# Two-block transformer kernel on one core: block 2's first norm with its mean taken off early and its squares summed as the output projection comes

## The reference

```python
mix = jnp.concatenate([a_out, b_out], axis=-1) @ w_o[i]
x = layer_norm(ALPHA * x + mix, ln1_g[i], ln1_b[i])
gate, up = jnp.split(x @ w_ffn_in[i], 2, axis=-1)
...
ple = (p[i] @ w_ple[i]) * jax.nn.sigmoid(x @ w_ple_gate[i])
x = layer_norm(ALPHA * x + ffn + ple, ln2_g[i], ln2_b[i])
...
def layer_norm(x, g, b):
    mu = jnp.mean(xf, axis=-1, keepdims=True)
    var = jnp.mean(jnp.square(xf - mu), axis=-1, keepdims=True)
    y = (xf - mu) * lax.rsqrt(var + LN_EPS)
```

## Time and profile before

| | us |
|---|---|
| median of 3 runs (2494.79 to 2498.84) | 2498.53 |
| profiled execution, its own time | 2500.13 |
| its span in the trace | 2498.3 |
| PE busy | 2424.8 (97%) |
| DVE busy | 1765.1 (71%) |
| ACT busy | 1095.0 (44%) |
| POOL busy | 1065.5 (43%) |
| granted TensorE clock, mean | 0.992 |

### The profile page before, as it was taken

One profiled execution on the slowest core, in us unless ns is written; L12 is line 12 of the kernel. 1 busy time (PEld: TensorE's weight loads), 2 busy tenths in 40 slices (PEclk: granted clock), 3 DMA queues, 4 the chain that ended last, 5 costly groups with the idle time before them and its releaser, 6 DMA issues.

```text
span 2498.3 us, 35167 instructions
## 1 busy us (share of the span) xinstructions
PE 2424.8 (97%) x13615; PEld 2033.0 (81%) x13615; DVE 1765.1 (71%) x2671; ACT 1095.0 (44%) x1803; POOL 1065.5 (43%) x600
## 2 busy tenths in 40 slices
PE   6999999999999999999999999999999999999997
PEld 4777788988777788998777779999877777999985
DVE  4677777864477787774597478887468747888746
ACT  4325532434426543443444555444444355444442
POOL 0323553434234244544254446544515534755441
PEclk8999999999999999999999999999999999999998
DMA  8613345553322433332232113332223212333221
GB/s 288 203 51 123 114 152 169 189 164 110 95 85 85 135 118 119 102 102 85 86 85 76 55 64 127 108 104 92 95 82 85 76 51 68 102 124 105 94 87 49
DMA packets 239645, 268.87 MB, mean 108 GB/s; under 512 B 19976, under 2 KB 204024, under 8 KB 239224
## 3 DMA queue, kind: packets, MB, share of 16 engines
q1 hardware_dynamic: 239480, 266.63, 33.1%
HBM read 264.51 MB, written 2.10 MB: 107 GB/s over the span
## 4 chain that ended last, share of the span: by engine, by line
PE 75%; DVE 10%; issue 5%; ACT 4%; POOL 3%; DMA 3%; SPq 1%; ACTq 0%; DVEq 0%; POOLq 0%
PE bank L2801 22%; PE bank L2803 22%; PE bank L2802 22%; DVE k_lo L2057 1%; DMA raw<-in_w_ffn_in 1%; DVE r L1908 1%; POOL w_lo L1652 1%; POOL k_lo L1663 1%; DMA raw<-in_ffn_w 1%; ACT k_hi L1105 1%; DVE u_sum L2074 1%; PE bank L3404 1%; PE bank L3470 1%; DVE u_t_raw L2087 1%; PE bank L3130 1%
## 5 line engine op out<-in xcount | busy, mean ns | idle before, releaser
L1663 POOL TENSOR_TENSOR k_lo<-raw,k_hi 128x512 fp32r<-128x512 f32 x297 | 430.0, 1459 | 542.9 <-ACT k_hi L1105 541.9
L1652 POOL TENSOR_TENSOR w_lo<-raw,w_hi 128x2048 fp32r<-128x2048 f32 x53 | 248.8, 4694 | 525.3 <-ACT w_hi L1051 446.3
L1105 ACT ACTIVATE k_hi<-raw 128x512 fp32r<-128x512 f32 x444 | 270.9, 626 | 310.7 <-PE bank L2803 249.4
L2801 PE MATMUL bank<-h_hi,k_lo 128*128 128x256 f32 (+1 forms) x1156 | 370.8, 321 | 3.8 <-DVE k_lo L2057 2.5
L2802 PE MATMUL bank<-h_lo,k_hi 128*128 128x256 f32 (+1 forms) x1156 | 369.6, 320 | 0.0
L2803 PE MATMUL bank<-h_hi,k_hi 128*128 128x256 f32 (+1 forms) x1156 | 369.5, 320 | 0.0
L2801 PE MATMUL bank<-h_hi,w_lo 128*128 128x512 f32 x800 | 325.0, 406 | 10.7 <-DVE h_lo L2017 3.9
L2803 PE MATMUL bank<-h_hi,w_hi 128*128 128x512 f32 x800 | 313.4, 392 | 0.0
L2802 PE MATMUL bank<-h_lo,w_hi 128*128 128x512 f32 x800 | 313.3, 392 | 0.0
L2801 PE MATMUL bank<-f_hi,k_lo 128*128 128x512 f32 x704 | 278.4, 395 | 8.6 <-DVE u_row L2118 2.9
L2801 PE MATMUL bank<-u_t_hi,k_lo 128*128 128x256 f32 x1008 | 282.6, 280 | 1.2 <-POOL k_lo L1663 1.2
(11 more groups left out here) (401 smaller groups left out, 4929.6 us busy)
## 6 DMA issues: line engine op xcount, KB each, us to landing
raw<-in_ffn_w SPq DMA_DIRECT2D x56, 1024.0 KB, 5.4
raw<-in_w_ffn_in SPq DMA_DIRECT2D x44, 1024.0 KB, 5.1
raw<-in_w_in SPq DMA_DIRECT2D x34, 1024.0 KB
b_raw<-in_ada_w SPq DMA_DIRECT2D x32, 1024.0 KB, 5.2
f_raw<-in_w_ffn_out SPq DMA_DIRECT2D x24, 512.0 KB, 3.4
z_a<-in_ada_w SPq DMA_DIRECT2D x4, 2048.0 KB, 14.1
g_raw<-in_ada_w SPq DMA_DIRECT2D x8, 1024.0 KB, 5.6
raw<-in_w_out SPq DMA_DIRECT2D x8, 1024.0 KB
```

The source lines that it names most:

```text
L1105: act.activation(hi, src, ACT.Copy).then_inc(s.f_hi.up, 1)
L1652: pool.tensor_tensor(b.w_lo[p][:, 0:n], b.raw[p][:, 0:n], b.w_hi[p][:, 0:n].bitcast(F32), ALU.subtract)\
L1663: pool.tensor_tensor(lo, src, hi.bitcast(F32), ALU.subtract).then_inc(s.f_lo.up, 1)
L2801: pe.matmul(out, wlo, xhi, start=start, stop=False)
```

## The change

Three things change in each layer of block 2.

1. DVE adds up the eight tiles of `x` before the last half of the output projection comes (`dve_early_shift`, seven additions), PE sums that over channels right behind the first channel tile of `attended(0)`, and DVE takes this provisional mean off all eight tiles; only then come the additions of the projection's tiles.
2. ACT squares each tile as soon as its addition is done, between its splits 14 and 15. PE sums the squares of tiles 0 to 3 between output tiles 6 and 7, those of 4 to 6 behind tile 7, and that of tile 7 at the end.
3. The variance is the mean square less the squared mean: ACT squares the mean, DVE subtracts, ACT goes on with `Ln` and `Exp`. The remaining mean is taken off tile by tile between the scalings.

```diff
@@ act_layer_norm
-    for k in range(KD):
-        act.wait_ge(*s.ld(l, k + 1))
-        act.activation(b.sq[:, k, :], b.x[:, k, :], ACT.Square).then_inc(s.lsq.up, 1)
     act.wait_ge(*s.lmean(l, 2))
-    act.activation(b.r[:, :], bank[7][:, :], ACT.Ln, bias=b.eps[:, 1:2], scale=1.0 / D).then_inc(s.l_r.up, 1)
-    act.wait_ge(*s.l_r(l, 1))
+    act.activation(b.sq[:, 1, :], bank[6][:, :], ACT.Square, scale=1.0 / D).then_inc(s.l_r.up, 1)
+    act.wait_ge(*s.var(l, 1))
+    act.activation(b.r[:, :], b.sq[:, 1, :], ACT.Ln, bias=b.eps[:, 1:2]).then_inc(s.l_r.up, 1)
+    act.wait_ge(*s.l_r(l, 2))
     act.activation(b.r[:, :], b.r[:, :], ACT.Exp, scale=-0.5).then_inc(s.l_r.up, 1)
     act_normed(act, e, l * 2, 0)
+
+def act_square_out(act, e, l, ks):
+    s, b = e.s, e.b
+    for k in ks:
+        act.wait_ge(*s.res(l, k + 1))
+        act.activation(b.sq[:, k, :], b.x[:, k, :], ACT.Square).then_inc(s.lsq.up, 1)
@@ act_layer2
     split(14)
+    act_square_out(act, e, l, range(KD))
     split(15)
     act_layer_norm(act, e, l)
@@ dve_layer_norm
-    dve.wait_ge(*s.lmean(l, 1))
-    for k in range(KD):
-        dve.scalar_tensor_tensor(b.x[:, k, :], bank[6][:, :], -1.0 / D, b.x[:, k, :], ALU.mult, ALU.add)\
-           .then_inc(s.ld.up, 1)
-    dve.wait_ge(*s.l_r(l, 2))
-    for k in range(KD):
-        dve.wait_ge(*s.ld(l, k + 1))
+    dve.wait_ge(*s.l_r(l, 1))
+    dve.wait_ge(*s.lmean(l, 3))
+    dve.scalar_tensor_tensor(b.sq[:, 1, :], bank[7][:, :], 1.0 / D, b.sq[:, 1, :], ALU.mult, ALU.subtract)\
+       .then_inc(s.var.up, 1)
+    for k in range(2):
+        dve_less_mean(dve, e, k, -1.0 / D)
+    dve.wait_ge(*s.l_r(l, 3))
+    for k in range(KD):
+        dve.wait_ge(*s.ld(l, KD + k + 1))
         dve_scaled(dve, e, k)
         if k == 0:
             dve_normed(dve, e, l * 2, 0)
+        if k + 2 < KD:
+            dve_less_mean(dve, e, k + 2, -1.0 / D)
...
+def dve_less_mean(dve, e, k, part):
+    s, b = e.s, e.b
+    dve.scalar_tensor_tensor(b.x[:, k, :], e.bank[6][:, :], part, b.x[:, k, :], ALU.mult, ALU.add)\
+       .then_inc(s.ld.up, 1)
+
+def dve_early_shift(dve, e, lay, l):
+    s, b = e.s, e.b
+    for k in range(2):
+        dve.wait_ge(*lay.bank_out(k % 2, PART_USE[KD - 2 + k]))
+    dve.tensor_tensor(b.r[:, :], b.x[:, 0, :], b.x[:, 1, :], ALU.add).then_inc(s.lsum.up, 1)
+    for k in range(2, KD):
+        dve.wait_ge(*s.lsum(l, k - 1))
+        dve.tensor_tensor(b.r[:, :], b.r[:, :], b.x[:, k, :], ALU.add).then_inc(s.lsum.up, 1)
+    dve.wait_ge(*s.lmean(l, 1))
+    for k in range(KD):
+        dve_less_mean(dve, e, k, -1.0 / D)
@@ dve_layer2
     c = l * 2
+    dve_early_shift(dve, e, lay, l)
     for k in range(KD):
+        dve.wait_ge(*s.ld(l, k + 1))
         dve.wait_ge(*(s.att(l, 3 * (k // 4) + k % 4 + 1) if k % 4 < 3 else
                       s.tile(lay.pair(6), k // 4, 1)))
-        dve.wait_ge(*lay.bank_out(k % 2, PART_USE[k]))
@@ pe_layer_norm
-    pe.wait_ge(*s.lsum(l, 6))
+    pe_square_sums(pe, e, l, range(4, KD - 1))
+    pe.wait_ge(*s.lsum(l, 13))
+    pe.wait_ge(*s.ld(l, KD))
     pe.matmul(bank[6][:, :], b.ones[:, :], b.r[:, :], start=True, stop=False)
     pe.wait_ge(*s.res(l, KD))
     pe.matmul(bank[6][:, :], b.ones[:, :], b.x[:, KD - 1, :], start=False, stop=True).then_inc(s.lmean.up, 1)
-    for k in range(KD):
+    pe_square_sums(pe, e, l, (KD - 1,)).then_inc(s.lmean.up, 1)
+
+def pe_square_sums(pe, e, l, ks):
+    s, b = e.s, e.b
+    for k in ks:
         pe.wait_ge(*s.lsq(l, k + 1))
-        op = pe.matmul(bank[7][:, :], b.ones[:, :], b.sq[:, k, :], start=(k == 0), stop=(k == KD - 1))
-    op.then_inc(s.lmean.up, 1)
+        op = pe.matmul(e.bank[7][:, :], b.ones[:, :], b.sq[:, k, :], start=(k == 0), stop=(k == KD - 1))
+    return op
@@ pe_layer2, attended
                     if k == 3:
                         op.then_inc(*((s.att.up, 1) if m < 3 else (s.half.up, 2)))
+                if k == 0:
+                    pe.wait_ge(*s.lsum(l, KD - 1))
+                    pe.matmul(bank[6][:, :], b.ones[:, :], b.r[:, :], start=True, stop=True).then_inc(s.lmean.up, 1)
...
                 op.then_inc(*((s.att.up, 1) if m < 7 else (s.half.up, 2)))
+                if m == 6:
+                    pe_square_sums(pe, e, l, range(4))
```

More of the change, by code:

```diff
@@ L598, in __init__ @@
         self.gn_m, self.v_m = in_turn("gn_m_v_m", 2, 1)
-        self.gn_x, self.lsum = in_turn("gn_x_lsum", 2, 6)
+        self.gn_x, self.lsum = in_turn("gn_x_lsum", 2, 13)
         self.cn_x, self.wi = in_turn("cn_x_wi", 2, 1)
@@ L639, in __init__ @@
         self.v_n = up("v_n", 4)
-        self.lmean = up("lmean", 2)
-        self.ld = up("ld", 8)
-        self.l_r = up("l_r", 2)
+        self.lmean = up("lmean", 3)
+        self.ld = up("ld", 2 * KD)
+        self.l_r = up("l_r", 3)
         self.n2_sum = up("n2_sum", 3 + 6)
@@ L646, in __init__ @@
         self.n2_r = up("n2_r", 3)
-        self.n2_var = up("n2_var", 1)
+        self.var = up("var", 2)
         self.lxr = up("lxr", KD + 1)
@@ L1401, in act_shift_norm @@
     act.activation(b.f_full[:, 1, :], bank[6][:, :], ACT.Square, scale=1.0 / D).then_inc(s.n2_r.up, 1)
-    act.wait_ge(*s.n2_var(l, 1))
+    act.wait_ge(*s.var(l, 2))
     act.activation(b.r[:, :], b.f_full[:, 1, :], ACT.Ln, bias=b.eps[:, 1:2]).then_inc(s.n2_r.up, 1)
@@ L2479, in dve_add_up @@
     else:
-        dve.wait_ge(*s.lsum(l, k - 1))
+        dve.wait_ge(*s.lsum(l, k + 6))
         dve.tensor_tensor(b.r[:, :], b.r[:, :], b.x[:, k, :], ALU.add).then_inc(s.lsum.up, 1)
@@ L2542, in dve_shift_norm @@
     dve.scalar_tensor_tensor(b.f_full[:, 1, :], bank[7][:, :], 1.0 / D, b.f_full[:, 1, :], ALU.mult, ALU.subtract)\
-       .then_inc(s.n2_var.up, 1)
+       .then_inc(s.var.up, 1)
     for k in range(2):
```

## The result

| | before | changed |
|---|---|---|
| median of the compared runs, us | 2497.75 (4 runs) | 2518.26 (4 runs, 2516.99 to 2521.16) |
| ratio | | 1.0086, 95% interval 1.0068 to 1.0103 |
| profiled execution, its own time, us | 2500.13 | 2518.86 |
| its span, us | 2498.3 | 2517.1 |

The change makes the kernel 20.5 us slower. The forecast was 23.1 us slower, 2521.6; the range was 2509 to 2528. The profiled spans differ by 18.8 us only: the changed execution reached the norm 2.7 us earlier than the one before (DVE's last probabilities start at 1405.3 against 1408.0), which is nothing that the change does. I therefore compare stretches inside each execution, not start times.

A forecast was written before the change was run, and what follows sets the result against it. The prediction took PE, busy 97% of the span, as the bound. Per layer 7.1 + 1.7 + 3.4 - 0.65 = 11.55 us, 23.1 for two, giving 2521.6 us against the 2498.5 median; range 2509 to 2528.

The forecast's parts named there:

- Term A: At attended(0), PE waits for DVE's seven additions, held up by POOL, then sums: 7.1 us a layer, 6.1 idle.
- DVE wins the last turn: Rival: addition 7 enters before POOL's split 13, PE idles 1.7 us, the early sum costs 2.8; 2509.6 us; chance 0.06.
- POOL does not hold the additions up: Rival: the seven additions end before PE asks, leaving 0.95 us for the sum; 2501.9 us in all; chance 0.06.
- Term B: Behind PE's wait for the early sum, the lower clock costs 1.7 us a layer (1.7 or 2.5 possible).
- Term C: Four sums of squares on PE ahead of output tile 7, 0.86 us each: 3.4 us a layer.
- Term D: From last projection matmul to the gate's second channel tile: gain of 0.65 us a layer, 2.2 without clock loss.
- The norm itself pays: Rival: the square sums and early sum find idle PE slots, leaving a 2.65 us gain a layer; 2493.2 us; chance 0.03.

The follow-up runs named there:

- Experiment 2: Changed kernel with 25 discarded matmuls in front of PE's wait for the early sum: 2515.65 us, ratio 1.007.
- Experiments 1: Changed kernel with the running sum of the early additions in a PSUM bank, so all but the first have one SBUF input: 2506.17 us, ratio 1.0035.
- experiment 9: experiment 8 with ACT writing the inverse root into PSUM bank 7, from where DVE scales: 2490.07 us, ratio 0.9972.
- experiment 11: experiment 10 with the early mean back, gathered in PSUM and summed on PE behind the second channel tile: 2492.26 us, ratio 0.9979.
- experiment 4: Changed kernel with PE's early sum behind the third channel tile of attended(0) instead of the first: 2504.42 us, ratio 1.003.
- experiment 6: Changed kernel without early additions, early sum or early subtraction; squares are of x with its mean in it: 2501.49 us, ratio 1.0016.
- experiment 8: Changed kernel without early mean, split 15 before tile 7's square, fp32r square sums, 26 discarded matmuls ahead of the wait replacing 19 behind: 2491.80 us, ratio 0.9975.
- experiment 7: Kernel before, with squares written as fp32r and summed with fp32r ones, one pass instead of two: 2495.83 us, ratio 0.9993.
- experiment 10: experiment 9 with each h_lo earlier in DVE's list, ahead of later mean subtractions, and 20 discarded matmuls instead of 26: 2490.94 us, ratio 0.9971.
- experiment 5: Changed kernel with ACT's split 15 ahead of the square of tile 7 instead of behind it: 2518.61 us, ratio 1.0085.
- experiments 3: Changed kernel with all eight sums of squares behind output tile 7, none ahead of it: 2517.36 us, ratio 1.0078.

## Why the prediction was right, point by point

**Term A, the early sum (7.1 forecast): right, and shown.** The wait is 5.62 us (6.1 forecast), released by DVE's last addition, in both layers. The turns came out one by one as worked from the earlier trace rows: additions 3, 4, 6 and 7 were held, 1, 2 and 5 were not. Experiment 2, where the clock stays up, has the term alone: 23.46 us from the twelfth projection matmul to the slot behind tile 6 instead of 16.55, so 6.91. Addition 7 lost its turn to split 13, so the rival *DVE wins the last turn* fell. Experiments 1 and 9 show that POOL is the cause. That rules out the rival *POOL does not hold the additions up*, and with it the narrow reading of the Trainium skill's "Advanced Engine Details and Errata", section "VectorE Performance Modes". Another page of the Trainium skill, "SBUF — State Buffer", section "Who interferes with whom", says that a DVE instruction with two SBUF inputs contends with a GpSimd instruction that reads SBUF, and one with at most one SBUF input, outside the 2-port modes, does not. The trace agrees on both: 1.65 to 4.98 us against 0.7.

**Term B, the clock behind it (1.7 forecast): right in kind, too small.** Experiment 2 gives 2.45 and 2.68 us in the trace, about the upper of my bounds; I had taken the value of a shorter stretch. The slow time did begin while PE was still idle (granted clock 0.50 from 1420.4, the sum starts at 1421.98), but 5.1 us of it were left for the matmuls. A and B together were forecast at 8.8. From the twelfth projection matmul to the slot behind tile 6 they cost 9.24 us in the first layer (25.79 instead of 16.55) and 9.47 in the second.

**Term C, four sums ahead of tile 7 (3.4): right.** Tile 7 is 3.44 us later in the trace. Up to the first matmul behind the sums it is 3.03 us; another 0.4 passes because the second fp32r matmul behind them comes 0.63 us after the first, not 0.23. Together that is the four times 0.86. The early sum costs the same where PE doesn't wait for it: in experiment 11 the stretch from the twelfth projection matmul to the slot behind tile 6 takes 17.45 us instead of 16.55, so 0.90, and for that part of term A I had 0.96. In experiment 4 it takes 18.02, so 1.47, because there PE still waits: the sum starts at 1424.07, where the next projection matmul was due at 1423.61. The medians of experiments 4 and 6 differ by 2.9, 1.5 a layer.

**Term D, the tail (gain of 0.65 forecast): mis-sized.** It gained 2.29 and 2.27 us in the two layers of the profiled execution. The step that failed is "I take 1.7 us for it", the lower clock behind the idle stretch of 2.85. The stretch came (2.80), the lower clock did not, and without it I had worked out 2.2. The other kernels show why neither value is the answer: behind the same stretch the clock fell in five of ten layers, for 1.3 to 1.6 us each. By these ten layers the right term is a gain of about 1.5 us on average, an estimate, with both values in the range. What decides between the two stays open.

**The sum.** In the profiled execution 9.24 + 3.44 - 2.29 = 10.4 us in the first layer and 10.6 in the second, 21.0 for two; the medians differ by 20.5. Forecast 23.1: 1.6 a layer too much in D, 0.5 too little in A and B. The two errors have opposite signs, so part of the closeness is luck. By whole runs it comes apart like this: squares and tail alone 4.0 us (experiment 6), the early sum with next to no wait 2.9 more (experiment 4), the wait 11.2 more (experiment 2), the clock 2.6 more (changed kernel), with some of D's chance in each figure.

**The norm itself pays** was the rival with a gain. Experiment 6 puts the norm without its early mean at 4 us slower, so it falls as stated: the sums found no idle slots. It is the price of the sums on PE that decides: with sums at a quarter of the price, split 15 ahead of the last square and the idle stretch filled, the norm without its early mean is 5.7 us faster than the kernel before (experiment 8), while the old form gains nothing certain by them (experiment 7).

**The best version** of these is experiment 9, 2490.07 us, ratio 0.9972; 8 and 10 can't be told from it. With the early mean kept, it is experiment 11, 0.9979. All four sum the squares in fp32r, with the lower precision that experiment 7 names.

## What to carry to other kernels

Before work is moved under another engine's work, look at where its inputs lie and what GpSimd does at that time: a chain of VectorE operations with two SBUF inputs can take three times its length, and one input in PSUM frees it. Put a wait on an in-order engine only where the last thing that it waits for is certain to be done; two channel tiles later, the same slow additions cost their sum and a wait of 0.30 us. When one part gets earlier, ask what other engines then start earlier, and what that runs into (experiment 10). And an idle stretch of PE of 2.3 to 2.9 us has had two prices here, with and without the lower clock behind it: carry both.

## What the runs showed of the hardware that I had not expected

- Behind an idle stretch of 2.73 to 2.81 us in one and the same place the granted clock fell in five of ten layers, in some executions in one layer and not in the other. Behind 2.32 and 2.33 us at another place it fell in three of four (experiments 10 and 11). Behind 1.55 and 1.56 us it stayed at 1.00 (experiment 5), and in a wait of 5.59 to 5.63 it fell in all six layers of the changed kernel and of experiments 3 and 5 (the early sum behind it took 2.07 or 2.08 us instead of 1.12).
- The clock also fell with no idle stretch of that length at all: in experiment 7, where PE started a short matmul every 0.6 us with pauses between them, it was 0.62 during the sums.
- A `tensor_scalar` with one SBUF input and its output in SBUF, 0.55 us alone, took 0.95 and ended 0.27 us behind POOL's operation (experiment 9), as the two-input operations do with 0.55. The Trainium skill's page "SBUF — State Buffer", section "Who interferes with whom", lists `tensor_scalar` among the operations that can take the ports which DVE and GpSimd share; the trace agrees. `scalar_tensor_tensor` with a PSUM input was not held up (0.69 for one and 1.28 for two beside POOL in experiment 9).
- Behind an fp32 sum the second of the fp32r matmuls comes 0.63 us after the first instead of 0.23. The first starts only 0.03 us after the sum's second pass, so this is no price on top of the sum's 0.86 us.
